# A decoder layer with expert lookup: the sample tokens' channel and gate products join the third span's

## The chip, the cores and the metric

The kernel runs on one core of one Trainium2 chip. The metric is device microseconds of one execution; the runs shown give a median of 3741.41 us. The core has five engines with their own instruction queues: TensorE (PE in the profile), VectorE (DVE), ScalarE (ACT), GpSimd (POOL) and SyncE (SP). Sixteen DMA engines move data between DRAM and the core's memory.

## The reference

One layer of a hybrid decoder for 1024 prompt tokens (behind 16 meta tokens) and 32 sample tokens (8 sequences of 4). All data are float32, the width is 1024.

```python
h = rmsnorm(x)
[B | C | xin | q_lat | kv_lat | k_rope | gate_conv | gate_attn] = h @ w_in
y_c = w_conv_out(B * conv3_causal(C * xin))            # 512 channels, width 3
y_a = w_attn_out(concat heads)                         # prompt: causal; sample: over a paged cache
x = x + w_mix_out(sigmoid(gate_conv) * y_c + sigmoid(gate_attn) * y_a)
x = x + PEER(rmsnorm(x))
# PEER: 8 heads, product keys 128 x 128, top 16; each pick reads one row of peer_u and of peer_v
```

For the sample tokens the convolution's history comes from a saved state of two columns per sequence, and new states are outputs.

## The kernel before, in words

Two first stages compute the norm, the latents, queries, keys and values. All that matters here is in `tail_stage`. The tokens are cut into four spans (SPANS): prompt tokens 0 to 255, 256 to 639, 640 to 1023, and the 32 sample tokens. Each span c goes through

- attention (for the fourth span `decode()`: eight sequences, each with 8 cache pages turned, projected, asked and summed, then `values()`, the product of the latents with w_uv),
- 12 channel groups (CHAN: for each of 4 blocks of 128 channels the columns C, xin and B of w_in, 8 products of 128 x 128 weights each), out of which VectorE makes the convolution (`channels`),
- 8 merge blocks ob of four groups j: two gate groups (GATE, 8 products each), an output product of the convolution (CONV j = 2, 4 products) and one of the attention (j = 3, 4 products),
- 8 mix groups (MIX), the mean of squares, and the norm,
- 16 search heads (PROJ, SCORE), each followed on VectorE by a search for the 16 best keys.

Next to this runs, unit by unit, the expert lookup of the span before. A unit is one pick (of 128) of one tile of 128 tokens: POOL gathers 128 rows of 8 KB of the table (L848) into one of RING = 9 slots, VectorE multiplies the first half of the row with the token and sums (L1493), ScalarE applies Gelu and the weight (L1242, L1226), and the second half is added up either by TensorE (ScalarE builds a diagonal matrix, L1214; TensorE four matmuls of 512 columns, L917) or by VectorE (L1474); `by_dve(u)` says which. POOL issues unit u once the slot of u - 9 is free, which TensorE or VectorE signals. There are 8 x 128 + 32 = 1056 units. The first 32-token tile of sample tokens is folded over four quarters, hence 32 units.

How many units stand between two steps of a span is set by a table: TICK gives each step of a span a number of ticks, `passed` adds them up, and `due(c, i, lag)` turns step i into a unit number, in the fourth span 696 + 328 x 23/25 x (ticks passed)/(all ticks). All engines follow the same table; ScalarE runs 3 units ahead of TensorE, VectorE 6 (3 in decode), POOL as far as the ring lets it. Step 0 (MERGE) is the first gate group; the channel groups are steps -12 to -1. In the fourth span a unit goes to VectorE where u is odd, from the first channel group on where u is not a multiple of 4, and in the search where u % 8 is 7.

The weights come in groups of 512 KB (576 KB for a search head) through WRING = 3 slots, loaded by SP in the order of their use (`TailWeights.start`, L481). SP waits before each load until the products of three groups before are done. The value product's result is copied by ScalarE (L1318), stored to DRAM by it (`s_attn`, L1321, signal av_stored), and loaded by SP into YA (four loads, L820, signal ya_in) as the right side of the output products j = 3 (L1167); in the fourth span SP comes to these loads after the channel groups' weights.

Of the kernel before, what the change touches and what calls it, by code (L numbers as in the profile page):

```python
# [13 lines left out]
ALU = mybir.AluOpType  # L14
# [3 lines left out]
P = 128  # L18
D = 1024
KD = D // P  # L20
# [437 lines left out]
class TailWeights:  # L458
# [3 lines left out]
    GROUPS = CONV + 3 * KD + KD + HC  # L462

# [5 lines left out]
    def source(self, g):  # L469
# [9 lines left out]
    def start(self, sp, w):  # L479
        src, s = self.source(w % self.GROUPS), w % WRING  # L480
        sp.dma_start(self.tile[:, s, 0:src.shape[1], :], src).then_inc(self.arrived[s], 16)  # L481


def tail_stage(nc, K, X, H, weights, d):

    with ExitStack() as ctx:
# [38 lines left out]
        with ExitStack() as decoding:  # L525
# [12 lines left out]
            PG = sb("pages2", [P, NPG, KVL + ROPE], c=decoding)  # L538
        with ExitStack() as attending:
# [5 lines left out]
        CX = lambda o: room[:, o % 2 * 400:o % 2 * 400 + 2 + NMAX]  # L545
        CU, CY = room[:, 800:800 + 2 + NMAX], room[:, 1200:1200 + NMAX]
        US = room[:, 1600:1600 + NSEQ * (2 + DSEQ)].rearrange("p (s q) -> p s q", q=2 + DSEQ)
# [12 lines left out]
        OLAT = sb("olat", [P, KT, NH, NSEQ, DSEQ])  # L560
        AS = sb("as", [VH, NH, NS])
# [35 lines left out]
        conv_in, conv_step, conv_stored = (sem(n) for n in ("conv_in", "conv_step", "conv_stored"))  # L597
# [17 lines left out]
        for c in range(NCH):  # L615
# [20 lines left out]
            order += [(c, CHAN, g) for g in range(NCV)]  # L636
            order += [(c, GATE if j < 2 else CONV, ob * 4 + j) for ob in range(KD) for j in range(4)]
# [18 lines left out]
        def last_use(w):  # L656
            c, g = divmod(w, GROUPS)
            if g < NCV:
                return ready[c, CHAN, g]
# [3 lines left out]
            if g < 4 * KD:  # L663
# [13 lines left out]
        PRE = [len(x) + 5 + NCV for x in items] + [DEC + NCV]  # L677
# [13 lines left out]
        EDGE = [56, begin[1] + 40, begin[2] + 56, begin[3]]  # L691

# [12 lines left out]
        def by_dve(u):  # L705
# [3 lines left out]
            for c in range(NCH):  # L709
                if u < due(c, END, 0):  # L710
                    if u >= due(c, RANK, 0):
                        return u % 8 == 7
                    return u % 4 != 0 if u >= due(c, -NCV, 0) else u % 2 == 1
# [19 lines left out]
        def _(sp):  # L733
# [73 lines left out]
            for c, (a, n) in enumerate(SPANS):  # L807
                for g in range(GROUPS):
                    w = c * GROUPS + g
# [7 lines left out]
                    if g == NCV and c == NCH - 1:  # L817
# [7 lines left out]
            sp.wait_ge(dve_took, dve_count[NCH - 1, CHAN, NCV - 1])  # L825
# [58 lines left out]
        def _(pe):  # L884
# [59 lines left out]
            def scores(c, q, a, n):  # L944
                bank_free(c, SCORE, q)
                pe.wait_ge(act_took, act_count[c, PROJ, q])
                s = (c * GROUPS + NCV + 4 * KD + q) % WRING
# [110 lines left out]
            def decode():  # L1058
# [20 lines left out]
                units(due(c, -NCV, 0))  # L1079
# [56 lines left out]
            for c, (a, n) in enumerate(SPANS):  # L1136
# [5 lines left out]
                for g in range(NCV):  # L1142
# [828 lines left out]
```

## Time and profile before

| what | value |
|---|---|
| runs | 3736.62, 3741.41, 3747.70 us |
| profiled execution | 3732.16 us, span 3730.4 us |
| TensorE busy | 3143.7 us (84%) |
| VectorE busy | 2625.2 us (70%) |
| ScalarE busy | 1358.4 us (36%) |
| POOL busy | 1097.1 us (29%) |
| DMA | 1289.23 MB, mean 346 GB/s |
| mean granted TensorE clock | 0.893 |

The page gives busy times of the engines, a row of 40 slices of the span (digits are tenths), the traffic, the chain of waits that ended last, and groups of instructions. On TensorE one product in float32 is two matmuls in the records. A DMA share of about 1 means that packets keep all sixteen engines busy. Idle time of an engine counts only if others wait for it.

The stages of the fourth span lie in the trace as follows: decode from 2670 us on, the value product at 3207.8, channel groups 3210 to 3259, merge 3267 to 3378, mix from 3379, and the search to about 3560. The third span's channel groups begin at 1980.5 and its merge ends at 2284.

### The profile page before, as it was taken

What the parts mean: (1) busy time and instruction counts of PE and PEld (TensorE: products, weight loads), DVE (VectorE), ACT (ScalarE), POOL (GpSimd) and SP (SyncE); (2) the same over time, 40 slices, a digit from 0 to 9 for tenths busy, and PEclk for the clock granted to TensorE, in tenths of its full rate; (3) what the DMA queues carried; (4) which work ended last, traced back from release to release, by engine and by line L of the source; (5) the groups of instructions that cost most, each with busy time, mean ns of one, the idle gap of its engine ahead of it and who ended that gap; (6) DMA issues with size and microseconds to landing.
All of it is one profiled execution on the core that took longest, in us unless ns stands there. A gap on an engine that the chain in (4) does not pass through costs nothing.

```text
span 3730.4 us, 35287 instructions
## 1 busy us (share of the span) xinstructions
PE 3143.7 (84%) x10224; PEld 1772.7 (48%) x10224; DVE 2625.2 (70%) x5845; ACT 1358.4 (36%) x3982; POOL 1097.1 (29%) x1252
## 2 busy tenths in 40 slices
PE   7986898868899999577878898899688989798887
PEld 4423786424555555233444454445244545576531
DVE  3264115997677879977677767789977677756874
ACT  2222202358612233355663222334344444212343
POOL 0000001443233333333343333334333333323342
PEclk9996799978899999788889999999798899776899
DMA  2111346999999989899999999999999999999998
GB/s 105 51 44 43 98 151 235 413 385 400 374 408 419 419 346 362 330 407 402 396 421 419 419 418 420 406 420 399 387 399 391 355 394 376 393 393 419 419 421 368
DMA packets 237088, 1289.23 MB, mean 346 GB/s; under 512 B 45467, under 2 KB 62939, under 8 KB 101412
## 3 DMA queue, kind: packets, MB, share of 16 engines
q0 software_dynamic: 152064, 1107.36, 73.0%
q1 hardware_dynamic: 83108, 175.28, 13.3%
q10 hardware_dynamic: 1728, 4.39, 0.3%
q8 instruction: 80, 1.31, 0.1%
q14 instruction: 108, 0.88, 0.1%
HBM read 1273.53 MB, written 13.40 MB: 345 GB/s over the span
## 4 chain that ended last, share of the span: by engine, by line
PE 32%; DMA 24%; DVE 23%; ACT 6%; issue 5%; POOL 1%; SPq 0%; DVEq 0%; POOLq 0%; ACTq 0%
DMA tl_uv<-in_uv,tl_idx 21%; PE tl_y L917 10%; DVE tl_uv L1493 8%; PE tl_f L1167 7%; DVE tl_acc L1474 4%; PE tl_f L1147 3%; PE tl_f L1195 3%; PE tl_f L1178 2%; PE tl_f L978 2%; PE tl_f L1091 1%; DMA w_tail<-in_w_merge 1%; PE tl_f L1114 1%; PE tl_f L1042 1%; POOL tl_uv L848 1%; DMA w_tail<-in_w_conv 1%
## 5 line engine op out<-in xcount | busy, mean ns | idle before, releaser
L848 POOL DMA_INDIRECT tl_uv<-in_uv,tl_idx x1056 | 1049.8, 994 | 1923.2 <-PE tl_y L917 1181.2
L1493 DVE CUSTOM_DVE_ANT_0 tl_uv<-tl_uv,tl_h 128x1024 f32<-128x1024 f32 x1056 | 1267.6, 1215 | 441.7 <-DMA tl_uv<-in_uv,tl_idx 428.7
L917 PE MATMUL tl_y<-tl_uv,tl_diag 128*128 128x512 f32 (+1 forms) x2428 | 1286.2, 671 | 296.6 <-ACT tl_diag L1214 296.0
L917 PEld LDWEIGHTS tl_y<-tl_uv,tl_diag 128*128 128x128 f32 (+1 forms) x2428 | 477.2, 208 | 937.5 <-issue 464.6
L1242 ACT ACTIVATE tl_ge<-tl_a 128x1 f32<-128x1 f32 x1056 | 210.0, 199 | 1211.2 <-DVE tl_a L1493 1206.1
L1474 DVE SCALAR_TENSOR_TENSOR tl_acc<-tl_uv,tl_w,tl_acc 128x1024 f32<-128x1024 f32 x441 | 564.7, 1281 | 76.7 <-ACT tl_w L1226 76.7
L1226 ACT ACTIVATE tl_w<-tl_ge,tl_weight 128x1 f32<-128x1 f32 x1024 | 301.5, 294 | 33.3
L1167 PE MATMUL tl_f<-H,w_tail 128*128 128x384 f32 (+2 forms) x1024 | 273.7, 426 | 14.0 <-DMA w_tail<-in_w_merge 11.8
L1195 PE MATMUL tl_f<-H,w_tail 128*128 128x384 f32 (+2 forms) x1024 | 264.2, 413 | 9.5 <-DVE H L1795 9.5
L1214 ACT ACTIVATE tl_diag<-K,tl_w 128x128 f32<-128x128 f32 (+1 forms) x607 | 241.2, 397 | 38.1 <-PE tl_y L917 18.9
L1167 PEld LDWEIGHTS tl_f<-H,w_tail 128*128 128x128 f32 x1024 | 193.3, 212 | 103.7 <-issue 21.0
L1195 PEld LDWEIGHTS tl_f<-H,w_tail 128*128 128x128 f32 x1024 | 180.7, 195 | 105.5 <-issue 39.4
L860 POOL TENSOR_TENSOR tl_cand<-tl_tv 128x48 f32<-128x48 f32 (+5 forms) x128 | 33.8, 294 | 664.4 <-DVE tl_ti L1525 594.1
L1147 PE MATMUL tl_f<-H,w_tail 128*128 128x384 f32 (+2 forms) x768 | 202.0, 424 | 7.4 <-DMA w_tail<-in_w_conv 6.7
L1147 PEld LDWEIGHTS tl_f<-H,w_tail 128*128 128x128 f32 x768 | 142.1, 207 | 74.6 <-issue 13.7
L1178 PE MATMUL tl_f<-tl_m,w_tail 128*128 128x384 f32 (+2 forms) x512 | 139.2, 431 | 12.6 <-DVE tl_m L1784 11.8
L1167 PE MATMUL tl_f<-tl_ya,w_tail 128*128 128x384 f32 (+2 forms) x512 | 137.8, 424 | 3.5 <-DMA w_tail<-in_w_merge 3.5
L978 PE MATMUL tl_f<-H 128*128 128x512 f32 x256 | 138.9, 671 | 0.0
L1398 ACT ACTIVATE tl_gates<-tl_f 128x384 f32<-128x384 f32 (+2 forms) x64 | 24.9, 388 | 294.8 <-PE tl_f L1167 294.8
L1091 PE MATMUL tl_f<-w_tail,H 96*128 96x512 f32 (+4 forms) x192 | 92.2, 593 | 43.1 <-ACT tl_att_pT L1331 43.1
L1178 PEld LDWEIGHTS tl_f<-tl_m,w_tail 128*128 128x128 f32 x512 | 97.3, 215 | 57.6 <-issue 22.8
L1617 DVE TENSOR_REDUCE tl_root<-tl_sq 128x8 f32<-128x512 f32 x64 | 43.7, 682 | 111.3 <-ACT tl_sq L1267 111.3
(229 smaller groups left out, 3099.1 us busy)
## 6 DMA issues: line engine op xcount, KB each, us to landing
w_tail<-in_w_merge SPq DMA_DIRECT2D x96, 512.0 KB, 7.8
w_tail<-in_w_peer SPq DMA_DIRECT2D x64, 576.0 KB, 7.9
w_tail<-in_w_conv SPq DMA_DIRECT2D x48, 512.0 KB, 7.9
tl_uv<-in_uv,tl_idx POOLq DMA_INDIRECT x1056, 13.2
w_tail<-in_w_mix SPq DMA_DIRECT2D x32, 512.0 KB, 7.8
X<-in_cache SPq DMA_DIRECT2D x48, 128.0 KB
X<-in_x SPq DMA_DIRECT2D x8, 536.0 KB, 6.7
o_y<-tl_acc ACTq DMA_DIRECT2D x8, 512.0 KB, 7.1
```

The lines of the kernel that those rows point to most:

```text
L848: pool.indirect_dma_start(UV[:, u % RING, :], None, d["uv"], bass.IndirectOffsetOnAxis(ap=which, axis=0)).then_inc(landed[u % RING], 16)
L917: mm = pe.matmul(Y[0:m, half * 512:(half + 1) * 512], DG[:, (pe_count[u] - 1) % DIAGS, 0:m], UV[:, u % RING, D + half * 512:D + (half + 1) ...
L978: mm = pe.matmul(F[:, bank_of[c, KEYS_, g], :], keysT(k, j * P, P), WKV[:, k, :], start=(k == 0), stop=(k == KT - 1))
L1147: mm = pe.matmul(F[:, bank_of[c, CHAN, g], 0:halo + n], W[:, s, k, :], H[:, k, META + a - halo:META + a + n], start=(k == 0), stop=(k == K ...
L1167: mm = pe.matmul(F[:, j, 0:n], W[:, s, (CT if j == 3 else 0) + k, :], x, start=(k == 0), stop=(k == nk - 1))
L1178: mm = pe.matmul(F[:, ob % 3, 0:n], W[:, s, k, :], M[:, k, 0:n], start=(k == 0), stop=(k == KD - 1))
L1195: mm = pe.matmul(F[:, q % 2, 0:n], W[:, s, k, :], H[:, k, META + a:META + a + n], start=(k == 0), stop=(k == KD - 1))
L1214: act.activation(DG[:, v % DIAGS, 0:m], K[:, at:at + m], ACT.Copy, scale=WP[:, t % 2, i:i + 1]).then_inc(diag, 1)
L1226: act.activation(WP[:, t % 2, i:i + 1], GE[:, t % 2, i:i + 1], ACT.Copy, scale=g).then_inc(weighed, 1)
L1242: act.activation(GE[:, t % 2, i:i + 1], A[:, t % 2, i:i + 1], ACT.Gelu).then_inc(gelu, 1)
L1474: dve.scalar_tensor_tensor(ACC[:], v, w, ACC[:], ALU.mult, ALU.add).then_inc(used_dve, 1)
L1493: dve.tensor_tensor_reduce(UV[:, u % RING, 0:D], UV[:, u % RING, 0:D], HP[:], 1.0, 0.0, ALU.mult, ALU.add, A[:, t % 2, i:i + 1]).then_inc( ...
```

## The change

The third span's channel and gate products get 32 more columns on the right (`wide(c)`): H holds the sample tokens' columns right behind those of the third span. VectorE's `channels` of the third span works on both parts, the prompt's with the semaphore conv_step and the sample tokens' with own_step; the sample tokens' product B * conv goes to a tile of its own, YS, and the Tanh of their gates to SGS. `channels` and the gates are left out of the fourth span; its weight queue has 8 merge, 8 mix and 16 peer groups (`merge`, `mix`, `peer` in TailWeights). The tick table of the fourth span loses the channel and gate ticks, and the last step before the values gets 20 ticks instead of 8. SP loads YA right after the value weights. From the start of merge on, no longer of the channel groups, a unit goes to VectorE where u is not a multiple of 4 (`lead`). OLAT and AS move to room shared with other tiles.

```diff
     CONV = 3 * CT
     GROUPS = CONV + 3 * KD + KD + HC
+    FULL = len(SPANS) - 1
+    SHORT = KD + KD + HC
+    TOTAL = FULL * GROUPS + SHORT
...
+    def merge(self, c, ob, part):
+        return c * self.GROUPS + (self.CONV + 3 * ob + part if c < self.FULL else ob)
...
-            order += [(c, CHAN, g) for g in range(NCV)]
-            order += [(c, GATE if j < 2 else CONV, ob * 4 + j) for ob in range(KD) for j in range(4)]
+            if c < NCH - 1:
+                order += [(c, CHAN, g) for g in range(NCV)]
+            order += [(c, GATE if j < 2 else CONV, ob * 4 + j) for ob in range(KD) for j in range(4) if c < NCH - 1 or j >= 2]
...
-        TICK.append([12, 9, 9, 10, 10, 11, 11, 16, 11] * NSEQ + [4, 4, 4, 6, 6, 4, 6, 8, 8] + [6] * NCV
-                    + [6, 6, 3, 3] * KD + [16] + [6] * KD + [16] + [12] * HC + [12] * 4 + [0])
+        TICK.append([12, 9, 9, 10, 10, 11, 11, 16, 11] * NSEQ + [4, 4, 4, 6, 6, 4, 6, 8, 20]
+                    + [0, 0, 3, 3] * KD + [16] + [6] * KD + [16] + [12] * HC + [12] * 4 + [0])
...
+        lead = lambda c: NCV if c < NCH - 1 else 0
+        wide = lambda c: SPANS[c][1] + (NS if c == NCH - 2 else 0)
...
                     if g == WRING and c == NCH - 1:
                         sp.wait_ge(ranked, c)
                         decode_loads()
-                    if g == NCV and c == NCH - 1:
                         sp.wait_ge(av_stored, 16)
                         for k in range(CT):
                             sp.dma_start(YA[:, CT + k, 0:n], d["s_attn"][2 * k:2 * k + 2, :, a:a + n].rearrange(
...
-                for g in range(NCV):
+                for g in range(lead(c)):
...
-                        mm = pe.matmul(F[:, bank_of[c, CHAN, g], 0:halo + n], W[:, s, k, :],
-                                       H[:, k, META + a - halo:META + a + n], start=(k == 0), stop=(k == KD - 1))
+                        mm = pe.matmul(F[:, bank_of[c, CHAN, g], 0:halo + wide(c)], W[:, s, k, :],
+                                       H[:, k, META + a - halo:META + a + wide(c)], start=(k == 0), stop=(k == KD - 1))
...
-                    for j in range(4):
+                    for j in range(0 if c < NCH - 1 else 2, 4):
...
+                        if c == NCH - 2:
+                            act.activation(SGS[:, ob, j, :], F[:, j, n:n + NS], ACT.Tanh, scale=0.5)
...
+                        own = 6 * o
+                        dve.tensor_copy(US[:, :, 0:2], STATE[:, o]).then_inc(own_step, 1)
+                        dve.tensor_tensor(US[:, :, 2:], by_seq(F[:, bank_of[c, CHAN, 3 * o + 1], n:n + NS]),
+                                          by_seq(CX(o)[:, 2 + n:2 + n + NS]), ALU.mult).then_inc(own_step, 1)
...
+                        dve.tensor_tensor(YS[:, o, :], CY[:, n:n + NS], F[:, bank_of[c, CHAN, 3 * o + 2], n:n + NS], ALU.mult)
```

SP's queue in the fourth span, from the load of the value weights on, before (a row is line, kind, what is written from what, the shape of one, the semaphores that it waits for, and a count):

```order
L765 DMA H<-in_w_uv 128x2x512 [waits tl_proj]
L481 DMA w_tail<-in_w_conv 128x1024 [waits tl_proj] x9
L820 DMA tl_ya<-s_attn 128x32 [waits tl_av_stored]
L820 DMA tl_ya<-s_attn 128x32 x3
L481 DMA w_tail<-in_w_merge 128x1024 [waits tl_proj] x24
L481 DMA w_tail<-in_w_mix 128x1024 [waits tl_proj] x8
L481 DMA w_tail<-in_w_peer 128x1152 [waits tl_proj] x16
```

And after the change, where L481 has become L496 and L820 L842:

```order
L788 DMA H<-in_w_uv 128x2x512 [waits tl_proj]
L842 DMA tl_ya<-s_attn 128x32 [waits tl_av_stored]
L842 DMA tl_ya<-s_attn 128x32 x3
L496 DMA w_tail<-in_w_merge 128x1024 [waits tl_proj] x5
L496 DMA w_tail<-in_w_mix 128x1024 [waits tl_proj] x8
L496 DMA w_tail<-in_w_peer 128x1152 [waits tl_proj] x16
```

Three groups are loaded ahead of decode in both (channel groups before, output groups after), so 12 + 24 became 3 + 5 = 8 groups. The loads of tl_ya stand directly behind the value weights.

TensorE from the end of decode on, before: units (L917), the value product (L1053), channel groups (L1147), the turn of the next token tile (L895), gate groups (L1167):

```order
L917 MATMUL tl_y<-tl_uv,tl_diag 128x512 x4
L1053 MATMUL tl_f<-tl_olat,H 64x32 x16
L1147 MATMUL tl_f<-H,w_tail 128x32 x8
L917 MATMUL tl_y<-tl_uv,tl_diag 128x512 x2
L1147 MATMUL tl_f<-H,w_tail 128x32 x24
...
L1147 MATMUL tl_f<-H,w_tail 128x32 x16
L895 MATMUL tl_h<-K,H 128x128 x8
L1167 MATMUL tl_f<-H,w_tail 128x32 x8
```

After the change, with waits (L939 was L917, L1075 was L1053, L1194 was L1167; tl_own_conv is YS):

```order
L939 MATMUL tl_y<-tl_uv,tl_diag 128x512 [waits tl_diag]
L939 MATMUL tl_y<-tl_uv,tl_diag 128x512
L1075 MATMUL tl_f<-tl_olat,H 64x32 [waits tl_dve_took,tl_wv_in]
L1075 MATMUL tl_f<-tl_olat,H 64x32 x15
L1194 MATMUL tl_f<-tl_own_conv,w_tail 128x32 [waits tl_dve_took,w_tail_in0]
L1194 MATMUL tl_f<-tl_own_conv,w_tail 128x32 x3
L1194 MATMUL tl_f<-tl_ya,w_tail 128x32 [waits tl_dve_took,tl_ya_in,w_tail_in0]
L1194 MATMUL tl_f<-tl_ya,w_tail 128x32 x3
L1194 MATMUL tl_f<-tl_own_conv,w_tail 128x32 [waits tl_dve_took,w_tail_in1]
```

Between the value product and the first wait for tl_ya_in stand four products, where 12 channel groups, two gate groups and an output group stood before. The turn of the token tile (L895) has moved ahead into decode.

## Rows read from the trace of the kernel before

**Rows 1.** The page's 40 slices (tenths, GB/s) and its traffic line.

```profile
DMA  2111346999999989899999999999999999999998
GB/s 105 51 44 43 98 151 235 413 385 400 374 408 419 419 346 362 330 407 402 396 421 419 419 418 420 406 420 399 387 399 391 355 394 376 393 393 419 419 421 368
DMA packets 237088, 1289.23 MB, mean 346 GB/s; under 512 B 45467, under 2 KB 62939, under 8 KB 101412
```

**Rows 2.** Stretches: us; PE, PEld, DVE, ACT, POOL busy; PEclk, DMA share, GB/s.

```profile
1980.00:2296.00 316.00, 266.45 (x731) 141.97 (x729) 239.67 (x338) 73.47 (x266) 101.95 (x106) 0.92 1.02 419
2670.00:3207.00 537.00, 460.33 (x1583) 258.53 (x1582) 407.39 (x670) 241.68 (x647) 186.32 (x185) 0.89 0.95 380
3207.00:3378.00 171.00, 150.73 (x709) 120.88 (x708) 101.03 (x174) 31.63 (x135) 51.25 (x51) 0.67 0.99 402
3378.00:3560.00 182.00, 156.93 (x606) 97.05 (x604) 138.80 (x410) 57.20 (x216) 65.00 (x96) 0.81 1.02 419
```

**Rows 3.** Waits of VectorE, 1980 to 2296: us, times, longest.

```profile
DVE tl_uv L1493 <- DMA tl_uv<-in_uv,tl_idx: 73.5, 65, 2.7
```

**Rows 4.** Waits of VectorE, then of POOL, 2670 to 3207 us.

```profile
DVE tl_root L1617 <- ACT tl_sq L1267: 111.3, 45, 9.4
DVE tl_uv L1493 <- DMA tl_uv<-in_uv,tl_idx: 0.7, 2, 0.5
POOL tl_uv L848 <- PE tl_y L917: 181.5, 55, 12.2
```

**Rows 5.** DMA issues, 3100 to 3400 us: KB each, us to landing.

```profile
w_tail<-in_w_merge SPq DMA_DIRECT2D x24, 512.0 KB, 8.9
s_attn<-tl_as ACTq DMA_DIRECT2D x1, 64.0 KB, 18.4
tl_ya<-s_attn SPq DMA_DIRECT2D x4, 16.0 KB, 13.7
```

**Rows 6.** Line 820 alone, the four attention loads.

```profile
DMA to landing us min/median/max: 10.4/13.7/16.9
```

**Rows 7.** Line 848, the gathers, 2670 to 3210 us: durations in ns.

```profile
L848 POOL DMA_INDIRECT tl_uv<-in_uv,tl_idx x187: 943/947/1933, 2670.7 to 3209.4; - x187
DMA to landing us min/median/max: 5.5/9.9/14.9
```

**Rows 8.** Lines 1147 (third span) and 978: duration ns min/median/max.

```profile
L1147 PE MATMUL tl_f<-H,w_tail x192: 486/486/847, 1980.9 to 2076.9; 128*128 128x384 f32 x192
L978 PE MATMUL tl_f<-H x256: 592/592/1222, 2689.5 to 3172.2; 128*128 128x512 f32 x128
```

**Rows 9.** Groups by form, 3200 to 3430 us: busy us, mean ns, idle before.

```profile
L1147 PE MATMUL tl_f<-H,w_tail 128*128 128x32 f32 x192 | 30.0, 321 | 4.8 <-DMA w_tail<-in_w_conv 4.1 <-ACT tl_as L1318 0.6
L1167 PE MATMUL tl_f<-H,w_tail 128*128 128x32 f32 x256 | 45.7, 345 | 12.0 <-DMA w_tail<-in_w_merge 11.8
L1398 ACT ACTIVATE tl_gates<-tl_f 128x32 f32<-128x32 f32 x16 | 3.2, 198 | 82.8 <-PE tl_f L1167 82.8
L1761 DVE SCALAR_TENSOR_TENSOR tl_m<-tl_m,tl_taps 128x32 f32<-128x32 f32 x8 | 2.0, 251 | 0.3
```

**Rows 10.** Chain of waits, 3200 to 3300 us: start, us, what.

```profile
3212.40 7.66 DMA w_tail<-in_w_conv
3220.10 3.63 PE tl_f L1147 x16
3248.81 18.71 DMA w_tail<-in_w_merge
```

**Rows 11.** In order of time: store of the values, its loads.

```profile
3210.32 0.68 ACTq L1321 DMA_DIRECT2D s_attn<-tl_as  x1
3245.42 1.85 SPq L820 DMA_DIRECT2D tl_ya<-s_attn  x4
```

**Rows 12.** TensorE in order of time, at either clock.

```profile
3186.25 3.35 PE L917 MATMUL tl_y<-tl_uv,tl_diag 128*128 128x512 f32 x4
3278.43 1.96 PE L917 MATMUL tl_y<-tl_uv,tl_diag 128*128 128x512 f32 x4
```

More of the change, by code:

```diff
@@ L467, in __init__, with mix, peer, source @@
         self.d = d
-    def source(self, g):
+    def merge(self, c, ob, part):
+        return c * self.GROUPS + (self.CONV + 3 * ob + part if c < self.FULL else ob)
+    def mix(self, c, ob):
+        return c * self.GROUPS + (self.CONV + 3 * KD if c < self.FULL else KD) + ob
+    def peer(self, c, q):
+        return self.mix(c, KD + q)
+    def source(self, w):
+        c, g = divmod(w, self.GROUPS)
+        if c == self.FULL:
+            g = self.CONV + (3 * g + 2 if g < KD else 2 * KD + g)
         if g < self.CONV:
@@ L657, in last_use @@
             c, g = divmod(w, GROUPS)
+            if c == NCH - 1:
+                g = NCV + (3 * g + 2 if g < KD else 2 * KD + g)
             if g < NCV:
@@ L807, in _ @@
             for c, (a, n) in enumerate(SPANS):
-                for g in range(GROUPS):
-                    w = c * GROUPS + g
+                for w in range(c * GROUPS, min((c + 1) * GROUPS, weights.TOTAL)):
+                    g = w - c * GROUPS
                     if g == 0 and c < NCH - 1:
@@ L1154, in _ @@
                         units(due(c, MERGE + i, 0))
-                        s = arrived(c * GROUPS + NCV + ob * 3 + min(j, 2))
-                        if i == 2:
+                        s = arrived(weights.merge(c, ob, min(j, 2)))
+                        if i == 2 and c < NCH - 1:
                             pe.wait_ge(dve_took, dve_count[c, CHAN, NCV - 1])
@@ L1172, in _ @@
                     units(due(c, MIXING + ob, 0))
-                    s = arrived(c * GROUPS + NCV + 3 * KD + ob)
+                    s = arrived(weights.mix(c, ob))
                     bank_free(c, MIX, ob)
@@ L1384, in _ @@
                 halo = 2 if c == 0 else 0
-                for o in range(CT):
+                for o in range(CT if c < NCH - 1 else 0):
                     units(due(c, 3 * o - NCV, LAG_ACT))
@@ L1730, in channels @@
             def channels(c, n):
-                halo, sample = (2 if c == 0 else 0), c == NCH - 1
+                halo, sample = (2 if c == 0 else 0), c == NCH - 2
+                by_seq = lambda z: z.rearrange("p (s q) -> p s q", q=DSEQ)
                 if c == 0:
@@ L1755, in channels @@
+                    dve.tensor_tensor(CU[:, 2 - halo:2 + n], x, gate, ALU.mult).then_inc(dve_took, 1)
+                    if sample:
+                        dve.wait_ge(own_step, own + 2)
+                        dve.tensor_copy(NEWS[:, o], US[:, :, DSEQ:]).then_inc(own_step, 1)
+                        dve.tensor_scalar(by_seq(CY[:, n:n + NS]), US[:, :, 0:DSEQ], tap(0), None, ALU.mult).then_inc(own_step, 1)
                     dve.wait_ge(conv_step, at + 1)
                     dve.wait_ge(dve_took, dve_count[c, CHAN, 3 * o + 1])
-                    dve.tensor_copy(kept, last).then_inc(conv_step, 1)
@@ L1758, in channels @@
-                    dve.tensor_scalar(y, part(0), tap(0), None, ALU.mult).then_inc(conv_step, 1)
+                    dve.tensor_copy(NEWP[:, o], CU[:, n:n + 2]).then_inc(conv_step, 1)
+                    dve.tensor_scalar(CY[:, 0:n], CU[:, 0:n], tap(0), None, ALU.mult).then_inc(conv_step, 1)
                     for k in (1, 2):
+                        if sample:
+                            z = by_seq(CY[:, n:n + NS])
+                            dve.wait_ge(own_step, own + 3 + k)
+                            dve.scalar_tensor_tensor(z, US[:, :, k:k + DSEQ], tap(k), z, ALU.mult, ALU.add).then_inc(own_step, 1)
```

75 lines of the change are left out of this document (39 added, 36 removed).

## The prediction

> **What bounds the kernel now.** I read the page's 40 slices first, then a table of five stretches, then the waits in them, and last the chain of waits around the place that changes. From slice 17 on the DMA row stands at 9 with 355 to 421 GB/s [rows 1]. By stretch [rows 2] the third span's channel, gate and output products (1980 to 2296 us) run at 419 GB/s with a DMA share of 1.02; the decode stretch of the fourth span (2670 to 3207) at 380 GB/s and 0.95; its channel, gate and output products (3207 to 3378) at 402 and 0.99; mix and search (3378 to 3560) at 419. TensorE is busy 84 to 88% in the same stretches and VectorE 59 to 76%, but who waits for whom tells: in the third span VectorE waits 73.5 us in 65 waits for gathered expert rows [rows 3]. So the bytes through the sixteen DMA engines set the time, and what matters of a change is how many bytes it takes away and how long it leaves the queues empty. The decode stretch is the exception: VectorE waits 0.7 us there for gathers and 111.3 us for ScalarE's squares [rows 4]; its engines lag, and 5% of the DMA time stays free.
>
> One gather unit is 128 rows of 8 KB, 1.049 MB, which is 2.50 us at 419 GB/s. One weight group is 0.524 MB, 1.25 us.
>
> **What goes.** The sample tokens had their own pass over 12 channel groups and 16 gate groups of weights; now the third span's pass does them, and the queue of weights in the fourth span has 8 output, 8 mix and 16 search groups (the order of SP, in the part on the change). 28 x 0.524 = 14.68 MB less, at 419 GB/s: **-35.0 us**. I take the rate of full stretches because the bytes go from stretches that are full [rows 2]. Their TensorE work, 30.0 + 45.7 us of matmuls on 32 columns [rows 9], goes too, and is worth nothing by itself as long as DMA is the bound; the weight loads that ended the waits of that stretch (7.66 us, 18.71 us in the chain [rows 10]) go with it.
>
> **What the third span gains.** 12 x 8 + 16 x 8 = 224 products, two passes each, 448 matmuls, widen from 384 to 416 columns. The medians at 384 and 512 columns are 486 and 592 ns [rows 8], 0.83 ns per column, so 448 x 32 x 0.83 ns = 11.9 us of TensorE in 316 us in which it is idle 50 [rows 2]. VectorE gets 28 small instructions, the longest kind 251 ns [rows 9], at most 7 us; ScalarE gets 16 small Tanh, 3.2 us [rows 9]. The 73.5 us that VectorE waits for gathers [rows 3] cover its part. TensorE's part holds back ring slots a little: nothing at least, 11.9 us at most. I take **+1**, near the row of VectorE's waits, since DMA stays at 1.02 only while nine slots hide what TensorE adds.
>
> **What the schedule moves.** The gather units are dealt out by ticks. Before, units 696 to 880 fall before the value product (842 of 1378 ticks, times 328 x 23/25); now 854 of 1222 ticks, so up to 906: 26 units more in decode and 26 fewer behind it. The trace's 187 gathers from 2670 to 3209 us agree with 184 [rows 7]. Behind decode they save 26 x 2.50 = 65 us, in full stretches. In decode they cost between 38 and 75 us: at most the stretch's mean, 537/187 = 2.87 us each; at least 65 less the 27 us that are free there (5% of 537). Net -27 to +10. The free time comes from TensorE blocking the ring for a fixed part of each sequence, the longest 12.2 us [rows 4], which more units don't remove, so I take **-4**, a sixth of it. The boundary between token tiles at unit 896, now within decode, was worth a dip in either place; I cost it at nothing.
>
> **The new wait.** The value product's result goes by ScalarE through a store to DRAM and back as the right side of the attention half of each output product. Before, the store went out at 3210.32 and landed after 18.4 us, the four loads were issued only at 3245.42 and needed 13.7 us [rows 5, 11]; 12 channel groups and 2 gate groups stood between. Now TensorE has the 4 products of the convolution half in between (8 matmuls, 2.8 us even at the mean of 345 ns [rows 9]), and then waits for the loads with everything behind it: its gather units 908 and on, and so POOL, which can issue up to unit 916. VectorE stops after product 912 for the same output product. Two sides: 18.4 + 1.9 + 16.9 us = 37 us if store and load take what they took with full queues (16.9 is the slowest of the four [rows 6]); 5.5 + 1.9 + 5.5 = 13 us if both land as fast as the quickest gather of the decode stretch [rows 7]. What counts is the time in which the DMA engines are empty. At the stop some 6 to 7 units are on the way or queued (nine slots, two or three landed), 15 to 17 us of work. I take it that the store lands while these drain, that the loads then have the queues for themselves, some 5 us as that quickest gather, and that 3 us pass until the first refilled slots flow: DMA empty **+8 us**, with 3 and 25 as ends (25: 37 - 16 + 4).
>
> The Trainium skill bears on the size of this. DMA: Bandwidth & Descriptors, section "Anatomy of one DMA", puts the fixed cost of a DMA at about 2 us, most of it the receipt for the write. By an estimate from that alone store and load would be over in some 5 us, the ring would cover all of it, and the sum would be 8 us lower. The Trainium skill's same page, section "Queues, rings and completion order", has each engine take turns between queues packet by packet, by which a store in many small packets is held up beside full gather queues. The 18.4 us for 64 KB beside 8.9 us for 512 KB [rows 5] speak for the second; no run here shows the first for this store.
>
> **The sum.** -35 + 1 - 4 + 8 = -30 us on the profiled execution: 3732.16 - 30 = 3702 us. That execution lies 0.25% below the median of the runs, 3741.41; in proportion the median comes to 3741.41 x 3702/3732 = **3711 us**, 0.8% faster.
>
> **Rivals.**
> *The decode stretch swallows more.* The 26 units fill most of the free 27 us there and the new wait is covered by the ring: -35 - 18 + 3 = -50, 3691 us. For it: VectorE has landed rows at hand there [rows 4]. Against: the stretch is at 0.95 already.
> *The wait eats most of it.* Store and load keep their loaded durations, 37 us, and the ring covers 16: DMA is empty for 25 us, -35 + 1 - 4 + 25 = -13, 3728 us. For it: the loads took 13.7 us with only 16 KB each [rows 5]. Against: by then nothing else is in the queues.
> *TensorE takes over (slower).* Place: the 16 search heads of the fourth span. After a stop of 20 us TensorE is at its lower level, and if it stays there the search is TensorE's. At that level four matmuls of a unit take 3.35 us instead of 1.96 and 16 matmuls on 32 columns 3.63 [rows 10, 12]. A head has 47/16 = 2.9 units, 7 of 8 on TensorE: 2.6 x 3.35 + 3.63 = 12.3 us against 3.67 MB / 419 = 8.8 us of DMA, 3.6 us lost per head (score products left out). It turns slower at the ninth head; 12 heads of 16 make +43, in all -35 + 1 - 4 + 8 + 43 = +13, 3754 us. The granted clock of 3207 to 3378, where 32-column products prevail, is 0.67, with DMA still at 0.99; in 3378 to 3560 it is 0.81 [rows 2]. In the merge and mix groups the same arithmetic gives 3.63 + 0.4 x 3.35 = 5.0 us of TensorE against (0.52 + 1.5 x 1.05) / 419 = 5.0 of DMA, so nothing is lost there. Against: a head's 2.6 units are dense matmuls, and the clock was on its way back before, 0.67 then 0.81 [rows 2]. The Trainium skill, TensorE: Matmul & The Clock Gate, section "What's actually happening", says that an idle array falls to 1.2 GHz and sustained work releases it; by that rule the clock is back after the first heads, and the sum doesn't change.
> That the change does nothing is excluded by the order: 28 loads are gone.
>
> **Chances.** Forecast 0.53 (its own range 3700 to 3724), first rival 0.13, second 0.24, third 0.10. A difference under 0.3% (11 us) is no change for a measurement of this kernel, so faster means under 3730 and slower over 3753. Faster: 0.49 of the forecast, all of the first, half of the second, 0.74. Same: 0.04 + 0.12 + 0.02 of the third = 0.18. Slower 0.08. The range goes from just under the first rival to well past the second, 3686 to 3741; what is left out is the third and the far ends of the others.
>
> **What will show it.** Traffic must fall from 1289 to about 1275 MB [rows 1]. The third span's stretch must stay at 419 GB/s and grow by 1 to 3 us, its 416-column matmuls at 0.51 us. Decode must hold some 210 gathers and take 590 to 605 us. Behind the value product I expect one wait of TensorE for the attention loads, 15 to 25 us, with a dip of DMA in it, then 79 units to the end of the heads at 419 GB/s. From the value product to the end of the search I expect 353 - 100 + 8 = 261 us. I am wrong if the dip is over 30 us, if third-span DMA falls under 1.0, or if decode grows by over 75 us.

## The result, and the profile after

The changed kernel takes 3685.28 us (median of 4 runs, 3674.68 to 3686.73) against 3739.01 us before in the same comparison; the ratio is 0.9834, with a 95% interval of 0.9813 to 0.9855. By the ratio that is 62 us less (54 to 70), twice the 30 us forecast; the two medians are 53.7 us apart, at the lower end of that interval. The median lies 0.7 us outside the forecast range. The profiled execution took 3686.73 us, 45 us less than that of before, which will turn out to have been a short one.

The page's rows after, for [rows 1]:

```profile
DMA  2111255999999998899999999999999999989998
GB/s 106 51 38 45 83 154 184 420 383 396 388 412 419 413 383 340 332 388 405 400 409 419 420 417 420 417 406 407 412 394 413 367 415 416 391 349 413 419 421 368
DMA packets 233053, 1274.50 MB, mean 346 GB/s; under 512 B 45019, under 2 KB 62491, under 8 KB 97380
```

The traffic is 14.7 MB less, as it must be. For [rows 2] the stretches after: third span (channel products to the end of merge), decode from the first key product to the value product, from there to the last search head, and the rest. Columns as in [rows 2].

```profile
1986.00:2290.00 304.00, 271.21 (x726) 140.33 (x724) 231.55 (x352) 71.88 (x271) 99.20 (x102) 0.94 1.02 419
2694.80:3254.60 559.80, 493.30 (x1645) 274.07 (x1643) 431.44 (x674) 252.52 (x696) 206.50 (x208) 0.89 0.99 400
3254.60:3491.70 237.10, 191.01 (x764) 128.44 (x764) 164.86 (x429) 64.38 (x242) 79.28 (x108) 0.73 0.97 395
3491.70:3684.90 193.20, 149.78 (x335) 46.82 (x334) 115.80 (x277) 70.90 (x243) 68.41 (x84) 0.98 0.95 396
```

Before, the same four marks lie at other places than the cuts of [rows 2], so here is the table again with these cuts (first key product 2689.5, value product 3207.8, last head 3544.3):

```profile
2689.50:3207.80 518.30, 451.05 (x1553) 252.24 (x1551) 390.24 (x614) 232.25 (x626) 183.97 (x182) 0.90 0.96 380
3207.80:3544.30 336.50, 293.47 (x1280) 212.45 (x1279) 224.02 (x529) 83.43 (x331) 107.56 (x132) 0.73 1.00 411
3544.30:3730.40 186.10, 144.57 (x327) 44.99 (x326) 112.61 (x274) 68.44 (x235) 68.14 (x85) 0.99 0.95 394
```

The third span's mix begins 316.0 us after its channel groups (before 315.6), and it still runs at 419 GB/s, so the wide products cost next to nothing. Decode grew by 41.5 us, not by 61, and runs at 400 GB/s where it ran at 380; by the prediction's own cut it takes 579 us, where 590 to 605 were forecast. From the value product to the last head it is 237.1 us instead of 336.5, 99 less and not 92. The rest takes 7 us more; by the tick table the heads end at unit 985 and no longer at 987, so 2 units more lie behind them. None of the three signs of being wrong that the prediction named came: the dip is 12 us, not over 30, the third span stays at 1.02, and decode grew by less than 75.

The wait for the DRAM trip, in order of time on TensorE, on the DMA queues of ScalarE and SP, and on POOL (start, duration, engine, what, idle before):

```profile
3254.61 2.05 PE L1075 MATMUL tl_f<-tl_olat,H 128*64 128x32 f32 x32
3256.60 1.08 PE L1194 MATMUL tl_f<-tl_own_conv,w_tail 128*128 128x32 f32 x8
3257.45 0.68 ACTq L1348 DMA_DIRECT2D s_attn<-tl_as  x1
3271.91 1.76 SPq L842 DMA_DIRECT2D tl_ya<-s_attn  x4
3275.02 1.89 PE L1194 MATMUL tl_f<-tl_ya,w_tail 128*128 128x32 f32 x8 [17.34 <-issue]
3282.46 0.94 POOL L870 DMA_INDIRECT tl_uv<-in_uv,tl_idx  x1 [22.14 <-PE tl_y L939]
```

And the landing times of the store, then of the four loads, where [rows 5] and [rows 6] had 18.4 and 10.4 to 16.9:

```profile
DMA to landing us min/median/max: 14.4/14.4/14.4
DMA to landing us min/median/max: 1.7/1.8/1.8
```

TensorE stood 17.3 us, POOL 22. The store took 14.4 us while the ring drained, the loads 1.7 to 1.8 us each, when the queues had run empty. What that cost the DMA engines is the stretch from 3262 to 3286, half empty: by its rate, 210 GB/s of 419, 12 us of 24, and by its share of 0.57 some 10:

```profile
3262.00:3286.00 24.00, 10.98 (x40) 8.95 (x40) 7.76 (x17) 1.89 (x7) 2.83 (x3) 0.50 0.57 210
```

For [rows 4], VectorE's waits in decode after. It waits for gathers now, 11.0 us where it was 0.7, and 20 us less for ScalarE's squares:

```profile
DVE tl_root L1646 <- ACT tl_sq L1294: 91.2, 39, 7.2
DVE tl_uv L1522 <- DMA tl_uv<-in_uv,tl_idx: 11.0, 14, 1.8
```

### The profile page after: what moved, and what is told of

It reads as the page before. It is cut to its first block, busy times and chain, and to the rows that moved or that the text cites. A ratio compares the mean times of both kernels' runs of the same rounds, so it can differ in the third digit from the quotient of the medians.

```text
span 3684.9 us, 34349 instructions
## 1 busy us (share of the span) xinstructions
PE 3113.5 (84%) x9808; PEld 1717.8 (47%) x9808; DVE 2613.8 (71%) x5837; ACT 1363.1 (37%) x3986; POOL 1090.7 (30%) x1252
## 4 chain that ended last, share of the span: by engine, by line
PE 33%; DMA 22%; DVE 22%; ACT 7%; issue 5%; POOL 1%; SPq 0%; DVEq 0%; POOLq 0%; ACTq 0%
DMA tl_uv<-in_uv,tl_idx 22%; PE tl_y L939 11%; DVE tl_uv L1522 8%; PE tl_f L1194 6%; DVE tl_acc L1503 4%; PE tl_f L1222 3%; PE tl_f L1169 2%; PE tl_f L1205 2%; PE tl_f L1000 2%; PE tl_f L1113 1%; POOL tl_uv L870 1%; PE tl_f L1064 1%; PE tl_f L1136 1%; ACT L1269 1%; ACT tl_att_s L1382 1%
## 5 line engine op out<-in xcount | busy, mean ns | idle before, releaser
L939 PE MATMUL tl_y<-tl_uv,tl_diag 128*128 128x512 f32 (+1 forms) x2460 | 1297.8, 670 | 304.2 <-ACT tl_diag L1241 286.8
L939 PEld LDWEIGHTS tl_y<-tl_uv,tl_diag 128*128 128x128 f32 (+1 forms) x2460 | 484.2, 208 | 962.5 <-issue 499.1
L1503 DVE SCALAR_TENSOR_TENSOR tl_acc<-tl_uv,tl_w,tl_acc 128x1024 f32<-128x1024 f32 x433 | 555.0, 1282 | 67.2 <-ACT tl_w L1253 66.2
L1222 PE MATMUL tl_f<-H,w_tail 128*128 128x384 f32 (+2 forms) x1024 | 267.4, 417 | 6.4 <-DVE H L1835 6.2
L1194 PE MATMUL tl_f<-H,w_tail 128*128 128x256 f32 (+2 forms) x768 | 235.2, 463 | 1.4 <-DVE tl_ya L1803 1.4
L1222 PEld LDWEIGHTS tl_f<-H,w_tail 128*128 128x128 f32 x1024 | 184.2, 200 | 102.3 <-issue 36.0
L1194 PEld LDWEIGHTS tl_f<-H,w_tail 128*128 128x128 f32 x768 | 147.3, 192 | 88.8 <-issue 49.6
L1169 PE MATMUL tl_f<-H,w_tail 128*128 128x258 f32 (+2 forms) x576 | 177.9, 469 | 3.0 <-DMA w_tail<-in_w_conv 3.0
L1169 PEld LDWEIGHTS tl_f<-H,w_tail 128*128 128x128 f32 x576 | 112.3, 195 | 70.5 <-issue 36.7
L1194 PE MATMUL tl_f<-tl_ya,w_tail 128*128 128x384 f32 (+2 forms) x448 | 129.0, 441 | 17.7 <-issue 17.3
L1194 PEld LDWEIGHTS tl_f<-tl_ya,w_tail 128*128 128x128 f32 x448 | 87.2, 208 | 60.9 <-issue 28.0
```

The costliest lines, as they stand in the source:

```text
L939: mm = pe.matmul(Y[0:m, half * 512:(half + 1) * 512], DG[:, (pe_count[u] - 1) % DIAGS, 0:m], UV[:, u % RING, D + half * 512:D + (half + 1) ...
L1169: mm = pe.matmul(F[:, bank_of[c, CHAN, g], 0:halo + wide(c)], W[:, s, k, :], H[:, k, META + a - halo:META + a + wide(c)], start=(k == 0), ...
L1194: mm = pe.matmul(F[:, j, 0:m], W[:, s, (CT if j == 3 else 0) + k, :], x, start=(k == 0), stop=(k == nk - 1))
L1222: mm = pe.matmul(F[:, q % 2, 0:n], W[:, s, k, :], H[:, k, META + a:META + a + n], start=(k == 0), stop=(k == KD - 1))
L1503: dve.scalar_tensor_tensor(ACC[:], v, w, ACC[:], ALU.mult, ALU.add).then_inc(used_dve, 1)
```

## The experiments

All ratios are to the kernel before, in runs on the same chip; 0.001 is 3.7 us. A difference between two of the ratios carries the intervals of both, some 9 to 12 us, and only what exceeds that is clear. "Decode" is from the first key product to the value product. Two theories stood against each other at first. Theory A: the 26 units were put where DMA time was free, and cost far less there than forecast. Theory B: the pace is worth 4 us, and the missing gain comes from the stretch that was taken out.

### The pace taken back, and the pace alone

`e1_old_pace`, from the changed kernel:

```diff
-[4, 4, 4, 6, 6, 4, 6, 8, 20] + [0, 0, 3, 3] * KD + [16] + [6] * KD + [16] + [12] * HC + [12] * 4 + [0]
+[4, 4, 4, 6, 6, 4, 6, 8, 8] + [0, 0, 3, 3] * KD + [16] + [6] * KD + [16] + [22, 23] * (HC // 2) + [12] * 4 + [0]
```

> The changed kernel with the old pace of units in decode (value product at unit 880 instead of 906; the ticks that are gone are put on the search heads instead, so the search ends at unit 987 as before). Theory A (the 26 units were put where DMA time was free, worth 20 us instead of the 4 forecast): 18 to 25 us slower than the changed kernel, decode back to 519 us, about 3705. Theory B (pace is worth 4 us as forecast, the missing 20 us come from the channel and gate stretch, which was worse than its bytes): within 6 us of the changed kernel.

`e2_pace_alone`, from the kernel before:

```diff
-[4, 4, 4, 6, 6, 4, 6, 8, 8] + [6] * NCV + [6, 6, 3, 3] * KD + [16] + [6] * KD + [16] + [12] * HC + [12] * 4 + [0]
+[4, 4, 4, 6, 6, 4, 6, 8, 8] + [4] * NCV + [4, 4, 2, 2] * KD + [11] + [4] * KD + [11] + [8] * HC + [8] * 4 + [0]
```

> The kernel before with nothing changed but its tick table: all steps behind the value product get about two thirds of their ticks, so that product stands at unit 907 instead of 880. Theory A: 15 to 25 us faster than before. Theory B: within 5 us of before.

The first gave 3715.55 us, ratio 0.9925 (0.9900 to 0.9950), 34 us slower than the changed kernel by the ratios (12 us either way) and 30 by the medians, where 18 to 25 were expected. The second gave 3719.95 us, ratio 0.9933 (0.9912 to 0.9954): a table of numbers alone makes the kernel before 25 us faster (17 to 33). Theory B falls. Taken in this order, the whole splits into 28 us for the work taken away (with the wait that it brought) and 34 us for the pace; in the other order it is 25 us for the pace and 37 for the work.

The three stretches from the first key product on, for `e1_old_pace` and then for `e2_pace_alone`:

```profile
2694.30:3226.60 532.30, 465.96 (x1553) 262.32 (x1551) 389.89 (x613) 233.68 (x628) 177.97 (x182) 0.87 0.94 370
3226.60:3526.80 300.20, 245.24 (x904) 151.30 (x904) 189.06 (x480) 86.26 (x318) 105.20 (x134) 0.81 0.96 393
3526.80:3725.90 199.10, 157.56 (x343) 50.08 (x342) 117.06 (x273) 72.98 (x251) 69.12 (x85) 0.96 0.96 398
2690.40:3253.40 563.00, 491.44 (x1646) 274.76 (x1644) 430.72 (x674) 252.79 (x695) 209.06 (x208) 0.90 0.99 400
3253.40:3538.50 285.10, 262.00 (x1185) 202.88 (x1184) 185.73 (x457) 62.70 (x259) 81.98 (x110) 0.69 0.98 395
3538.50:3719.50 181.00, 140.54 (x314) 44.12 (x314) 110.87 (x286) 66.54 (x232) 63.50 (x82) 0.97 0.95 390
```

Behind decode the changed kernel takes 430.3 us and `e1_old_pace` 499.3, so the 26 units saved 69 us there; from the kernel before (522.6 us) to `e2_pace_alone` (466.1 us) 27 units saved 57. The forecast's 65 lies between. One thing moves with the table: it also decides which engine adds up a unit. By the diagonal matrices that ScalarE builds for them, TensorE has 607 units before, 604 in `e2_pace_alone`, 615 in the changed kernel and 629 in `e1_old_pace`; so `e2_pace_alone` is the cleaner test of the two, and `e1_old_pace` may hold some of this shift. No run separates the two.

### Bytes alone, and products alone

`e4_bytes_alone`, from the kernel before, in `TailWeights.start`:

```diff
+        c, g = divmod(w, self.GROUPS)
+        if c == 3 and (g < self.CONV or g < self.CONV + 3 * KD and (g - self.CONV) % 3 < 2):
+            src = src[:, 0:1, :]
```

Each of the 28 loads brings 64 KB instead of 512, 12.8 MB less in all.

> The kernel before, with every instruction where it was, but the 28 weight loads of the fourth span's channel and gate groups cut to 64 KB each (12.8 MB less). Leaves out: the right weights in those products. Bytes theory: 12.8 MB / 419 = 31 us faster than before. Rival (that stretch is bound by TensorE at its lower clock and by the turn-taking of its steps, so bytes are worth less): under 20 us. If the weights' latency held it up on top: over 38 us.

`e9_bytes_kept`, from `e1_old_pace`, also in `start` (with a DRAM tensor s_spare of the size of a weight group, and a last wait for the copies at SP's end, not shown):

```diff
+        k = w - self.FULL * self.GROUPS - WRING
+        if 0 <= k < 28:
+            if k:
+                sp.wait_ge(self.spare_in, 16 * k)
+            sp.dma_start(self.spare, self.d["w_mix"][k % KD]).then_inc(self.spare_in, 16)
```

> The kernel of the first experiment (changed kernel, old pace in decode, 0.9925 of before), with 28 copies of 512 KB from DRAM to DRAM issued beside the fourth span's weight loads: the products of the channel and gate groups are gone, their bytes are back. Bytes theory: at 419 GB/s the copies cost 35 us, so it is 5 us slower than before to 5 us faster (the DRAM trip's dip included). Rival (TensorE at its lower clock was the bound of that stretch as much as DMA): more than 12 us faster than before.

Bytes alone: 3727.12 us, ratio 0.9952 (0.9937 to 0.9968), 18 us instead of 31, and the profile's stretch from the value product to the last head is 325.9 us, against 336.5 before and 338.8 in `e8_before_again`. Products alone: 3748.36 us, ratio 1.0009 (0.9991 to 1.0027), no net gain. This run also has the wait for the DRAM trip (TensorE stands 17.7 us), and beside the copies it waits 12.6 us for the mix and search weights, 0.8 before; so it doesn't show that the products are worth exactly nothing: with 8 to 12 us for the dip they would be worth some 5 to 9, an estimate within the noise. Against `e1_old_pace`, which differs from it by the copies alone, the bytes cost 31 us (12 either way) of the 35 that they are worth at 419 GB/s. So the bytes were the bound, but TensorE stood right behind it. The channel, gate and output products with the bytes gone, by stretch:

```profile
3222.00:3390.00 168.00, 162.06 (x716) 131.81 (x715) 107.87 (x188) 32.77 (x142) 52.99 (x52) 0.63 0.93 360
```

TensorE is busy 162 of 168 us, at a mean granted clock of 0.63, and DMA falls to 360 GB/s. Before, it was 150.7 of 171 us at 0.67 and 402 GB/s [rows 2]. Both removals together give about the 35 us (28, and the 8 to 12 of the wait), which is more than the 18 of the one and the little of the other.

### The DRAM trip taken out, units put into it, and the way on the chip

`e3_no_trip`, from the changed kernel (YT is a tile of its own; SP's wait for the store and its four loads of the result are gone, not shown):

```diff
-                            x = YA[:, (j - 2) * CT + k, 0:n]
+                            x = YT[:, k, :]
...
+                    sp.dma_start(YT[j * VH:(j + 1) * VH, k, :], d["s_q"][2 * k + j, 0:VH, 0:NS]).then_inc(ya_in, 16)
```

> The changed kernel, where the attention half of the sample tokens' output product takes other data (queries, loaded at the start into a tile of its own) and so never waits for the value product's way through DRAM; the store stays. Leaves out: the sample tokens' attention result. Dip theory (12 us of empty DMA queues, as the slices of the profile show, are lost for good): 10 to 14 us faster than the changed kernel, DMA at 419 GB/s behind the value product. Rival (the dip is made up for, since the ring is refilled while TensorE catches up, or the next weights are late instead): under 4 us.

3675.5 us, ratio 0.9812 (0.9790 to 0.9835); the ratios differ from the changed kernel's by 8 us, less than their noise and than the 10 to 14 expected, and the medians by 10. The profiles are clearer: from the value product to the last head it takes 223.5 us at 419 GB/s, against 237.1 in the changed kernel and 232.9 in `e5_narrow`, which has the same schedule and the trip:

```profile
3250.40:3473.90 223.50, 190.17 (x765) 126.42 (x764) 166.03 (x430) 65.04 (x244) 78.64 (x108) 0.76 1.02 419
3249.60:3482.50 232.90, 177.38 (x765) 118.23 (x764) 162.44 (x414) 63.72 (x241) 79.14 (x105) 0.79 0.97 395
```

So the dip is not made up for, with 8 to 14 us as its size.

`e6_units_in_wait`, from the changed kernel:

```diff
-[..., 8, 20] + [0, 0, 3, 3] * KD + [16] + ...
+[..., 8, 8] + [0, 0, 28, 3] + [0, 0, 3, 3] * (KD - 1) + [16] + ...
```

> The changed kernel with its pause moved: 7 gather units stand between the value product's first output product and the one that waits for the DRAM round trip (28 ticks there, 8 instead of 20 ahead of the values). Dip theory: the queues stay full during the 17 us wait, TensorE's wait falls under 6 us, and the kernel is 7 to 10 us faster than the changed one, near the 3675 of the run without the trip. Rival (the trip takes longer behind full queues, 18 + 14 us, and the wait moves instead of going): under 3 us.

3688.97 us, ratio 0.9847 (0.9829 to 0.9864): nothing gained. TensorE does four units (the other three are VectorE's) and still waits 14.84 us. The store landed after 6.8 us instead of 14.4, but the loads needed 7.5 to 14.0 us where they needed 1.7, with DMA at 348 to 415 GB/s around them; from the store's issue to the product that needs it are 22.3 us instead of 17.6. TensorE in order of time, then the landing of the loads:

```profile
3253.00 2.05 PE L1075 MATMUL tl_f<-tl_olat,H 128*64 128x32 f32 x32
3255.89 7.11 PE L939 MATMUL tl_y<-tl_uv,tl_diag 128*128 128x512 f32 x16
3277.84 1.89 PE L1194 MATMUL tl_f<-tl_ya,w_tail 128*128 128x32 f32 x8 [14.84 <-issue]
```

```profile
DMA to landing us min/median/max: 7.5/10.9/14.0
```

The rival's outcome came, though not by its numbers (18 + 14 us). With gathers in front of the loads the trip takes longer, and the DMA engines run half empty behind the wait instead of within it:

```profile
3278.00:3290.00 12.00, 12.00 (x46) 9.93 (x46) 6.03 (x14) 1.30 (x6) 3.79 (x4) 0.50 0.66 238
```

`e11_on_chip`, from the changed kernel:

```diff
-                for h in range(NH):
+                for g in range(CT):
                     for k in range(KT):
-                        mm = pe.matmul(F[0:VH, bank_of[c, VALUE, 0], h * NS:(h + 1) * NS], WKV[:, k, h * VH:(h + 1) * VH],
-                                       OLAT[:, k, h].rearrange("p s q -> p (s q)"), start=(k == 0), stop=(k == KT - 1),
+                        mm = pe.matmul(F[:, bank_of[c, VALUE, 0], 2 * g * NS:2 * (g + 1) * NS], WKV[:, k, g * P:(g + 1) * P],
+                                       OLAT[:, k, 2 * g:2 * g + 2].rearrange("p h s q -> p (h s q)"),
+                                       start=(k == 0), stop=(k == KT - 1),
...
+                v = F[:, bank_of[c, VALUE, 0], 0:NH * NS].rearrange("p (g h n) -> p g h n", h=2, n=NS)
+                act.activation(YT[0:VH], v[0:VH, :, 0], ACT.Copy)
+                act.activation(YT[VH:P], v[VH:P, :, 1], ACT.Copy).then_inc(act_took, 1)
```

> The changed kernel without the way through DRAM, and complete: the value product takes two heads' weights and two heads' latents at a time (8 products of 128 x 64 instead of 16 of 64 x 32), so that even heads come out on the lower and odd heads on the upper 64 partitions, and ScalarE copies the two halves into a tile of the output products. Dip theory: 8 to 12 us faster than the changed kernel, as the run without the trip was (3675.5 against 3685), with no wait of TensorE over 4 us there. Rival (what the run without the trip gained was its ready data): under 4 us.

3665.81 us, ratio 0.9801 (0.9781 to 0.9820). The medians put it 19 us ahead of the changed kernel, the ratios 12 (11 either way); each comparison has its own runs of the kernel before, so 12 is the better figure. TensorE behind the value product, which is now 16 matmuls of 64 columns and 1.89 us long:

```profile
3245.73 1.89 PE L1071 MATMUL tl_f<-tl_olat,H 128*128 128x64 f32 x16
3247.47 1.03 PE L1193 MATMUL tl_f<-tl_own_conv,w_tail 128*128 128x32 f32 x8
3248.33 1.06 PE L1193 MATMUL tl_f<-tl_own_attn,w_tail 128*128 128x32 f32 x8
3254.36 1.89 PE L1193 MATMUL tl_f<-tl_own_conv,w_tail 128*128 128x32 f32 x8 [4.97 <-DVE tl_own_gates L1819]
```

It goes straight through both halves of the first output product. One wait of 4.97 us is left, for VectorE's gates, a little over the 4 us expected. The whole way to the last head runs full, 220.4 us:

```profile
3245.70:3466.10 220.40, 189.17 (x748) 126.24 (x746) 162.27 (x410) 64.06 (x241) 77.10 (x104) 0.77 1.02 419
```

### How much a unit costs in decode

`e7_more_pace`, from the changed kernel, value product at unit 917:

```diff
-... + [16] + [6] * KD + [16] + [12] * HC + [12] * 4 + [0]
+... + [16] + [6] * KD + [16] + [9] * HC + [9] * 4 + [0]
```

> The changed kernel with 9 ticks instead of 12 for each search head and each of the four steps behind them, so that the value product stands at unit 917, 11 units more in decode. Saturation theory (decode at a DMA share of 0.99 has no free DMA time left): within 4 us of the changed kernel, decode longer by 25 to 28 us and the rest shorter by as much. Rival (a unit in decode still costs about 1.5 us instead of 2.5): 8 to 14 us faster.

`e10_less_pace`, from the changed kernel, value product at unit 853:

```diff
-[..., 8, 20] + [0, 0, 3, 3] * KD + [16] + [6] * KD + [16] + [12] * HC + ...
+[..., 8, 8] + [0, 0, 3, 3] * KD + [16] + [6] * KD + [16] + [37] * HC + ...
```

> The changed kernel with 37 ticks instead of 12 for each search head and 8 instead of 20 ahead of the values: the value product at unit 853, 53 units fewer in decode than the changed kernel has and 27 fewer than before. Theory A (below unit 906 decode is bound by the turn-taking of its steps, so units taken out of it shorten it by 1 to 1.4 us each and cost 2.5 us behind it): decode 490 to 508 us, 55 to 75 us slower than the changed kernel. Rival (DMA bound at any pace): decode about 430 us, total within 10 us of the changed kernel.

`e8_before_again` is the kernel before, unchanged.

> The kernel before once more, for one more profile of its decode stretch, which was 518 us from the first key product to the value product in its first profile and 519, 530 and 532 us in three experiments of the same pace. Theory A (the forecast took a short one for the rule): 525 to 533 us. Rival: 516 to 521.

`e12_on_chip_pace` has the edits of `e11_on_chip` and `e7_more_pace`.

> The on-chip version with 9 ticks for each search head and each of the four steps behind (value product at unit 917). Saturation theory: within 4 us of the on-chip version. Rival (the pace still pays, as the ratio 0.9813 against 0.9834 may say): 6 to 10 us faster than it.

More pace: 3678.69 us, ratio 0.9813 (0.9795 to 0.9831), 8 us under the changed kernel's ratio but with intervals that overlap; with the on-chip way the same step gives 3667.25 against 3665.81 us and 0.9793 (0.9773 to 0.9814) against 0.9801. Decode grew by 22 us, where 25 to 28 were expected. So the step is worth 0 to 8 us, and nothing clear. Less pace: 3732.36 us, ratio 0.9976 (0.9963 to 0.9989), 53 us behind the changed kernel, where 55 to 75 were expected. Before again: 3749.43 us in one run, decode 532.9 us, as expected.

Decode by the unit at which the value product stands:

| value product at unit | decode, us | us per unit moved in |
|---|---|---|
| 853 | 479.2 | |
| 880 | 518.3, 518.7, 530.5, 532.3, 532.9 (mean 526.5) | 1.75 |
| 906 (907 in `e2_pace_alone`) | 556.4, 556.5, 556.7, 559.8, 563.0 (mean 558.5) | 1.2 |
| 917 | 579.1, 582.2 (mean 580.7) | 2.0 |

The one profile left, `e6_units_in_wait` at unit 901, took 561.5 us, longer than those at 906. Profiles at one schedule differ by up to 14 us, and there is one at 853 and two at 917, so a price per unit is good to about 0.5 us. Up to 906 a unit costs 1.2 to 1.8 us in decode, beyond it 2.0. Behind decode a unit takes 2.50 us of DMA at 419 GB/s; measured, it saved 2.7 (`e1_old_pace` to the changed kernel), 2.1 (before to `e2_pace_alone`) and, for the last 11 units, 2.1 and 2.0 (to `e7_more_pace` and `e12_on_chip_pace`). So the last step saves behind decode just what it costs in it, and that is why it gains nothing.

The row at 906 stands above. The others are here, from `e10_less_pace` at 853:

```profile
2683.30:3162.50 479.20, 430.64 (x1502) 248.06 (x1500) 344.33 (x546) 214.37 (x558) 156.94 (x156) 0.89 0.91 354
```

from `e8_before_again` at 880:

```profile
2689.90:3222.80 532.90, 469.28 (x1554) 263.66 (x1552) 388.92 (x611) 233.79 (x627) 178.16 (x182) 0.87 0.93 370
```

and from `e7_more_pace` at 917:

```profile
2692.30:3274.50 582.20, 502.84 (x1666) 276.91 (x1664) 444.59 (x693) 258.03 (x715) 218.45 (x218) 0.90 0.99 401
```

The DMA share goes 0.91, 0.93, 0.99, 0.99 and the rate 354, 370, 400, 401 GB/s. VectorE's waits for gathers in decode go with it: at unit 880 they are 0.7 us, in `e1_old_pace` 0.2 and in `e8_before_again` none, while in `e2_pace_alone` (us, times, longest) they are

```profile
DVE tl_uv L1493 <- DMA tl_uv<-in_uv,tl_idx: 7.2, 10, 1.6
```

and in `e7_more_pace`

```profile
DVE tl_uv L1522 <- DMA tl_uv<-in_uv,tl_idx: 12.0, 18, 1.5
```

My number for the least pace was off: I expected 490 to 508 us of decode from a price of 1 to 1.4 us per unit, and it is 479.2; the price below 880 is nearer to 1.8. The rival, decode bound by DMA at any pace, is out: it asked for about 430 us.

### Without the sample tokens' columns

`e5_narrow`, from the changed kernel (SGS, YS and NEWS are filled with a constant once; VectorE's steps and ScalarE's Tanh for these columns are gone too, not shown):

```diff
-        wide = lambda c: SPANS[c][1] + (NS if c == NCH - 2 else 0)
+        wide = lambda c: SPANS[c][1]
```

> The changed kernel without the sample tokens' 32 columns in the third span: no wide products, no VectorE steps and no Tanh for them; constants stand in their place. Leaves out: the sample tokens' channel and gate values. Cover theory (11.9 us of TensorE and 6 us of VectorE lie beside a full DMA queue): within 3 us of the changed kernel (3685). Rival (they hold back ring slots): 6 to 12 us faster.

3679.53 us, ratio 0.9824 (0.9807 to 0.9842), 4 us under the changed kernel with intervals that overlap. The third span's mix begins 314.2 us after its channel groups, 1.7 us sooner. The 12 us of wider products are covered, save 0 to 4 us.

## Why the prediction was wrong

*What bounds the kernel.* Right in the main: taking the products away and leaving the bytes gained nothing net (1.0009, with the wait in it). It was too simple for the stretch that goes. "Worth nothing by itself as long as DMA is the bound" holds only with the bytes still there; with the products left and the bytes gone, TensorE is busy 96% of the stretch and part of the gain is held back (18 of 31 us). As both went, the term of -35 us came out within the noise: 28 measured with the wait in it, some 36 to 40 without. (The DMA row does not stand at 9 to the end, as I read it: its last slice is an 8, with 368 GB/s. Nothing rests on that.)

*The third span, +1.* Right: 0.4 to 1.7 us in the profiles, 0 to 4 by experiment. The wide matmuls took 512 ns, as forecast from 486 and 592.

*The pace, -4. This step failed*, and it is nearly all of the error. I said that the free time in decode "comes from TensorE blocking the ring for a fixed part of each sequence, which more units don't remove". The 26 units cost 32 us in decode (558.5 - 526.5), not 61, and saved 57 to 69 behind it, where 65 were forecast; with the table alone the kernel is 25 us faster, without it 34 slower. With -33 in place of -4 and 12 in place of 8 for the wait, the sum is -55, inside the 54 to 70 measured. The row that said so stood in my own list: VectorE waits 0.7 us for gathers and 111.3 for squares [rows 4]. That is a stretch in which rows lie landed and wait for their turn, as the tick table lets units through only as decode's steps advance. The busy times fit: from before to after TensorE's in decode grew by 42.2 us and VectorE's by 41.2, as much as the stretch itself (41.5). That this is the reason for the low price is read from the rows, and no run isolates it; the price itself is what the runs show. POOL's waits for TensorE hardly changed (181.5 us before [rows 4], 185.1 after), so the stops that I took for the cause are still there, but the free time that I tied to them is not: the rate rose from 380 to 400 GB/s. I also bounded the free time by the DMA share, 5% of one profile; the rate, 380 of 419 GB/s, would have said 9%, 49 us.

*The profiled execution was a short one.* Of five decode stretches at this pace two took 518 us and three 530 to 533. Their sequences differ by up to 5 us each, most of it in the last four, and the mean granted clock is 0.90 in the short ones, 0.86 to 0.87 in the long ones. So the 45 us between the two profiles understate what the runs show. Why some are short stays open.

*The new wait, +8.* Right in kind and order, low in size: the DMA engines lost 12 us. The store took 14.4 us, as expected while the ring drained; the loads were quicker than I took (1.7 us), and the refill slower, since POOL got its first slot 7 us after TensorE resumed, behind two output products and a unit at the lower clock. The Trainium skill (DMA: Bandwidth & Descriptors, "Anatomy of one DMA") gives its fixed cost of about 2 us for DMAs issued from GpSimd; these are SP's and ScalarE's. The loads in empty queues come near it, with 1.7 us each; the store behind gathers does not, with 13.9 to 19.1 us in eleven profiles and 6.8 in `e6_units_in_wait`. Why it was quick in that one is open.

*The rivals.* The first, decode swallows more, is what happened, with a chance of 0.13 and a time of 3691 us; its other half, the covered wait, did not. It priced the filled time at 18 us of gain, where the runs show 25 to 34. The second, 25 us of empty engines, is out. The third, TensorE at its lower clock in the search, did not come: the stretch to the last head ran at 0.73 as before, the heads themselves at 0.81 to 1.00 and 404 to 422 GB/s in three pieces from 3380 to 3491 us.

The best complete version is the changed kernel with the way on the chip: ratio 0.9801, or 0.9793 with more pace, which can't be told apart.

## What to carry to other kernels

Where two streams of work are dealt out by a table, look in each stretch at what the consumer waits for: if it never waits for the transfer, more of the other stream may fit in for less than its bytes cost elsewhere, as it did here up to unit 906. Try that table by itself before crediting a rewrite with the gain. And when two resources stand close, taking only one away can show half of the gain or none.

## What the runs showed of the hardware

A store of 64 KB in rows of 128 bytes took 13.9 to 19.1 us beside the gather queue in eleven of twelve profiles. The four loads of 16 KB took 1.7 to 1.8 us in queues that had run empty (the changed kernel, `e5_narrow`, `e10_less_pace`), 4.1 to 6.2 while the last gathers drained (`e1_old_pace`, `e7_more_pace`, `e9_bytes_kept`), and up to 17.2 behind gathers (`e8_before_again`).

In the stretch with 32-column products the mean granted clock was 0.67 before (TensorE busy 88% of it) and 0.63 in `e4_bytes_alone` (busy 96%), between its two levels of 1.2 and 2.4 GHz. In the changed kernel's search heads, 3380 to 3491 us, it was 1.00, 0.93 and 0.81 in three pieces.
